# Dense products in unsplit single precision instead of three reduced-precision products

## The reference

```python
def swiglu(h, w_gate, w_up, w_down):          # 1024 x 2816, 1024 x 2816, 2816 x 1024
    return (jax.nn.silu(h @ w_gate) * (h @ w_up)) @ w_down

for i in range(DEPTH):                        # DEPTH = 2
    x = x + 0.5 * swiglu(rmsnorm(x, ffn1_norm[i]), ...)
    x = x + mixer(rmsnorm(x, mix_norm[i]))    # gla: h @ w_in (1024 x 3088), attention, o @ w_out; sb: 1024 x 3072
    x = x + 0.5 * swiglu(rmsnorm(x, ffn2_norm[i]), ...)
# second block: h @ w_in (1024 x 3072), convolution and attention, @ w_out, then
for g in range(G):                            # 4 groups of 8 experts, 1024 x 512 each
    act = jax.nn.silu(hg) * hu * comb[:, g, :, None]
    y = y + jnp.einsum('tef,efd->td', act, w_down[g])
```

## Time and profile before

| | us |
|---|---|
| median of 3 runs | 1604.49 (1604.26 to 1605.66) |
| profiled execution | 1602.25 |
| its span, first to last instruction | 1600.5 |
| TensorE matmuls, busy | 1436.0 (90%) |
| VectorE busy | 885.6 (55%) |
| ScalarE busy | 625.0 (39%) |

### The profile page before, as it was taken

How to read it: one execution, slowest core, us unless ns; L and a number is a source line. 1 busy time by engine, 2 the same in 40 slices (tenths; PEclk the granted TensorE clock), 3 DMA queues, 4 the chain that set the end, 5 groups by cost and what they waited for, 6 DMA issues and landing times.

```text
span 1600.5 us, 23763 instructions
## 1 busy us (share of the span) xinstructions
PE 1436.0 (90%) x9182; PEld 1123.0 (70%) x9182; DVE 885.6 (55%) x1194; ACT 625.0 (39%) x832; POOL 31.0 (2%) x69
## 2 busy tenths in 40 slices
PE   7999999999999999999999999998786767767676
PEld 5888888888888888877788888777643433433433
DVE  4777678577776777665457776786521121121121
ACT  5443465564446434466554434664111011011010
POOL 4000000000000000000010000010000000000000
PEclk9999999999999999999999999999799898888978
DMA  7655543456564655653366554565999999999997
GB/s 220 210 187 197 190 161 132 133 182 211 175 202 148 207 200 171 209 171 119 109 186 210 195 198 158 168 201 224 372 399 416 419 417 417 419 418 417 419 417 309
DMA packets 170770, 396.63 MB, mean 248 GB/s; under 512 B 9508, under 2 KB 107892, under 8 KB 154337
## 3 DMA queue, kind: packets, MB, share of 16 engines
q1 hardware_dynamic: 169152, 392.20, 66.7%
q0 software_dynamic: 1440, 3.72, 1.0%
q10 hardware_dynamic: 128, 0.03, 0.0%
HBM read 393.83 MB, written 1.05 MB: 247 GB/s over the span
## 4 chain that ended last, share of the span: by engine, by line
PE 73%; DMA 11%; SPq 9%; DVE 3%; ACT 2%; issue 1%; DVEq 0%; ACTq 0%
PE psum L518 17%; PE psum L257 12%; PE psum L259 12%; PE psum L258 12%; DMA pair_ring<-in_w_exp_up 9%; PE psum L524 9%; SPq L2210 8%; PE psum L2262 4%; PE psum L2287 2%; PE psum L2306 1%; DMA pair_ring<-in_w_exp_down 1%; PE psum L985 1%; DVE low L252 1%; DVE hT L422 1%; PE psum L1396 1%
## 5 line engine op out<-in xcount | busy, mean ns | idle before, releaser
L252 DVE TENSOR_TENSOR low<-raw,high 128x2048 fp32r<-128x2048 f32 x179 | 409.6, 2291 | 194.2 <-ACT high L248 193.7
L248 ACT ACTIVATE high<-raw 128x2048 fp32r<-128x2048 f32 x179 | 341.3, 1910 | 125.7 <-PE psum L524 89.8
L518 PE MATMUL psum<-hT,high 128*128 128x512 f32 x1152 | 288.0, 392 | 2.0 <-DVE low L252 2.0
L518 PEld LDWEIGHTS psum<-hT,high 128*128 128x128 f32 x1152 | 209.2, 189 | 41.2 <-DVE low L252 2.2
L257 PE MATMUL psum<-high,hT 128*128 128x512 f32 x496 | 201.4, 406 | 8.6 <-DVE low L2546 5.0
L259 PE MATMUL psum<-high,hT 128*128 128x512 f32 x496 | 195.9, 395 | 0.0
L258 PE MATMUL psum<-low,hT 128*128 128x512 f32 x496 | 195.4, 394 | 0.0
L2287 PE MATMUL psum<-pair_ring,scratch 128*32 128x256 f32 x1984 | 139.4, 432 | 55.5 <-DMA pair_ring<-in_w_exp_up 55.4
L524 PEld LDWEIGHTS psum<-hT,low 128*128 128x128 f32 x1152 | 157.1, 190 | 11.3
L524 PE MATMUL psum<-hT,low 128*128 128x256 f32 x1152 | 160.6, 282 | 0.0
L2287 PEld LDWEIGHTS psum<-pair_ring,scratch 128*32 128x32 f32 x1984 | 66.9, 121 | 123.8 <-DMA pair_ring<-in_w_exp_up 68.7
(11 more groups left out here) (336 smaller groups left out, 1482.1 us busy)
## 6 DMA issues: line engine op xcount, KB each, us to landing
pair_ring<-in_w_exp_down SPq DMA_DIRECT2D x64, 1024.0 KB, 22.4
pair_ring<-in_w_exp_gate SPq DMA_DIRECT2D x62, 1024.0 KB, 22.1
pair_ring<-in_w_exp_up SPq DMA_DIRECT2D x62, 1024.0 KB, 22.8
raw<-in_ffn_w_gate SPq DMA_DIRECT2D x88, 512.0 KB, 4.0
raw<-in_ffn_w_up SPq DMA_DIRECT2D x88, 512.0 KB, 5.0
raw<-in_ffn_w_down SPq DMA_DIRECT2D x88, 512.0 KB, 4.3
raw<-in_gla_w_in SPq DMA_DIRECT2D x24, 512.0 KB, 4.5
raw<-in_sb_w_in SPq DMA_DIRECT2D x24, 512.0 KB, 4.7
```

What stands on the lines that cost most here:

```text
L248: act.activation(high[:, p % RING, :], raw_of(p), ACT.Copy).then_inc(rounded, 1)
L252: dve.tensor_tensor(low[:, p % RING, :], raw_of(p), high[:, p % RING, :].bitcast(F32), ALU.subtract).then_inc(split, 1)
L518: pe.matmul(to.rearrange("p (o n) -> p o n", o=2), w_high, both_parts, start=kk == 0, stop=False, skip_group_check=True)
```

## The change

- The type `fp32r`, the buffers `low` and `high`, the second halves of `hT` and `aT` and the split copies of the small weights are gone; two unused buffers keep the addresses behind them. `product` is one matmul in single precision that reads the landed piece.
- `raw` has six slots instead of three. Its loads wait on `used`, the end of the product six pieces before; TensorE waits for the landing of a piece itself. Loops over chunks take two chunks per pass, since six pieces make a round of the ring.
- Turning x: ScalarE writes the first four of eight columns, VectorE the other four, both from PSUM, instead of one after the other.
- The turned gate and up products write 256 columns and `block_norm` reads them from PSUM; copy and add are gone, and `block_gate` writes `aT` directly after waiting for the down products before.
- Experts: slots 0 to 2 lie in space that is free early, the other three wait for pieces 176, 178 and 180; a wait for a pair is one for each of its two DMAs; result adds and stores are made in halves of 512 columns.

```diff
-RING = 3
+RING = 6
+UNROLL = RING // 3
-        low = sb("low", [P, RING, SLOT], F32R)
-        high = sb("high", [P, RING, SLOT], F32R)
         raw = sb("raw", [P, RING, SLOT])
+        spare = sb("spare", [P, SPARE, SLOT])
...
         def piece_loads(sp, p, r, parts):
             if p >= RING or not isinstance(r, int):
-                sp.wait_ge(split, p - RING + 1 + scales_with(r, 3))
+                sp.wait_ge(used, p - RING + 1 + scales_with(r, RING))
...
-        def round_piece(act, p, r=0):
...
-        def split_piece(dve, p, r=0):
...
-        def product(pe, psum_out, lhs_high, lhs_low, rhs_high, rhs_low, start, stop=False):
-
-            pe.matmul(psum_out, lhs_high, rhs_high, start=start, stop=False, skip_group_check=True)
-            pe.matmul(psum_out, lhs_high, rhs_low, start=False, stop=False, skip_group_check=True)
-            return pe.matmul(psum_out, lhs_low, rhs_high, start=False, stop=stop, skip_group_check=True)
-
+        def piece_there(pe, p, r=0):
+            pe.wait_ge(*landed_of(p, r))
+
+        def product(pe, psum_out, lhs, rhs, start, stop=False):
+            return pe.matmul(psum_out, lhs, rhs, start=start, stop=stop, skip_group_check=True)
...
         def x_turn_act(act, k, tt):
...
+            x_turned(act, k, tt, 0)
+            for kk in range(4):
...
         def x_turn_dve(dve, k, tt):
...
+            x_turned(dve, k, tt, 1)
+            for i in range(4):
...
         def gate_up_turned_pe(pe, q, half, c):
...
-                both_parts = hT[:, :, kk * TOKENS:(kk + 1) * TOKENS]
...
             for k in range(4):
                 kk = 4 * half + k
                 for i in range(2):
-                    _, w_low, to = block(k, i)
-                    ins = pe.matmul(to[:, 0:TOKENS], w_low, hT_high[:, kk, :], start=False, stop=kk == KD - 1,
-                                    skip_group_check=True)
+                    cols = slice(i * CHUNK + c * P, i * CHUNK + (c + 1) * P)
+                    ins = product(pe, BLOCK[c][:, i * BANK:i * BANK + TOKENS], four_k(q)[:, k, cols], hT[:, kk, :],
+                                  start=kk == 0, stop=kk == KD - 1)
...
-            def block_sum(n, counter, value, lows):
+            def block_norm(n, counter, value, inner_free):
                 dve.wait_ge(counter, value)
                 if n == 0:
-                    dve.wait_ge(a_low, lows)
+                    dve.wait_ge(a_ready, inner_free)
                 parts = BLOCK[n].rearrange("p (w i n) -> p w i n", w=2, i=2)
...
+            def block_gate(n, number, down_done):
                 dve.wait_ge(block_silu, number + n)
...
+                if n == 0:
+                    dve.wait_ge(used, down_done)
+                ins = dve.tensor_tensor(aT[:, n, :], inner_sb[:, n, 0:TOKENS], inner_sb[:, n, TOKENS:2 * TOKENS], ALU.mult)
...
             for i in range(PAIRS):
-                if i == 1:
-                    sp.wait_ge(split, MOE)
-                elif i == 3:
-                    sp.wait_ge(used, MOE)
+                if i >= 3:
+                    sp.wait_ge(used, MOE - 10 + 2 * i)
                 pair_load(sp, i, 0, i // 3)
...
                 for tt in range(TT):
-                    dve.wait_ge(e["scattered"], b * TT + (tt + 1))
-                    dve.tensor_tensor(x[:, tt, :], SPREAD_Y[tt], x[:, tt, :], ALU.add).then_inc(e["added"], 1)
+                    for j in range(2):
+                        c = slice(j * BANK, (j + 1) * BANK)
+                        dve.wait_ge(e["scattered"], b * 2 * TT + (2 * tt + j + 1))
+                        dve.tensor_tensor(x[:, tt, c], SPREAD_Y[tt][:, c], x[:, tt, c], ALU.add).then_inc(e["added"], 1)
```

More of the change, by code:

```diff
@@ L440, in first_products, with tail_act @@
                 products(j, 1)
-        def tail_act(act, k, first, second, between):
-            round_piece(act, first)
+        def tail_act(act, k, between):
             if k == 7:
@@ L496, in gate_up_pe @@
             for k in range(4):
-                if isinstance(q, int) and q == 0 and tt == 0 and k == 2:
-                    pe.wait_ge(split, 1)
                 kk, tok = 4 * half + k, slice(tt * P, (tt + 1) * P)
-                ins = product(pe, GU[tt], hT_high[:, kk, tok], hT_low[:, kk, tok], four_k(high, q)[:, k, :],
-                              four_k(low, q)[:, k, :], start=kk == 0, stop=kk == KD - 1)
+                ins = product(pe, GU[tt], hT[:, kk, tok], four_k(q)[:, k, :], start=kk == 0, stop=kk == KD - 1)
             if tt == 1:
@@ L592, in first @@
             def first(half, tt):
-                if b + half == 0 and tt == 0:
-                    pe.wait_ge(first_split, 1)
-                else:
-                    pe.wait_ge(split, b + half + 1)
+                piece_there(pe, b + half)
                 gate_up_pe(pe, b + half, half, tt)
@@ L1268, in gla_dve @@
             diff(2)
-            piece(6)
             keep(0)
@@ L1281, in gla_dve @@
             diff(6)
-            piece(8)
             keep(4)
@@ L1321, in gla_dve @@
                 dve.tensor_tensor(v, v, proj[:, tt, 2560:3072], ALU.mult).then_inc(h_ready, 1)
-            piece(14)
-            for tt in range(TT):
-                low_half(tt, 1)
+            turned_tile(1, 1)
             out_dve(dve, "gla_out", 2)
@@ L1770, in mix_act @@
                                bias=eps[:, :]).then_inc(m["root"], 1)
-            piece(14)
-            for tt in range(TT):
-                high_half(tt, 1, tt + 3)
+            turned_tile(1)
             out_act(act, "mix_out", 8)
@@ L1902, in mix_dve @@
             dve.wait_ge(used, b + IN_PIECES)
-            for tt in range(TT):
-                low_half(tt, 0, tt + 1)
-            piece(13)
+            turned_tile(0)
             for tt in range(TT):
@@ L1918, in mix_dve @@
                 ins.then_inc(h_ready, 1)
-            piece(14)
-            for tt in range(TT):
-                low_half(tt, 1, tt + 3)
+            turned_tile(1)
             out_dve(dve, "mix_out", 8)
@@ L2149, in products @@
                 for k in range(4 * half, 4 * half + 4):
-                    tok = slice(tt * P, (tt + 1) * P)
-                    pe.matmul(ROUTE[:, tt * 2 * n:(tt + 1) * 2 * n], hT_high[:, k, tok],
-                              router_parts[:, k, :, :].rearrange("p i n -> p (i n)"), start=tt == 0 and k == 0, stop=False,
-                              skip_group_check=True)
-                    ins = pe.matmul(ROUTE[:, tt * 2 * n:tt * 2 * n + n], hT_low[:, k, tok], router_high[:, k, :],
-                                    start=False, stop=False, skip_group_check=True)
+                    ins = product(pe, ROUTE[:, tt * n:(tt + 1) * n], hT[:, k, tt * P:(tt + 1) * P], router[:, k, :],
+                                  start=tt == 0 and k == 0, stop=k == KD - 1)
                 if half == 1 and tt == 1:
@@ L2280, in gate_up @@
                         pe.wait_ge(e["x_sb"], at(b, 2, half + 1))
-                    pair_there(pe, i, b)
+                    for part in range(2):
+                        half_there(pe, i, b, part)
                     w = pair(i, b).rearrange("p (w k n) -> p w k n", w=2, k=4)
```

520 lines of the change are left out of this document (164 added, 356 removed).

## The result

The changed kernel takes 1830.05 us (median; 1828.99 to 1833.01) against 1604.61 for the kernel before, a ratio of 1.1407 (95% interval 1.1387 to 1.1426): 14% slower. The forecast was 1833, in a range of 1816 to 1862. The profiled span is 1828.4 us; the prediction's sum gave 1828.7. That nearness is partly luck: two of its terms were wrong, in opposite directions. (The other 3 us of the forecast are the step from span to median: the profiled execution had been 2.2 us under the median before, and is level with it now.)

What follows compares the result with a forecast made beforehand. TensorE was taken to bound the dense part, weight loads the experts' part. Span 1600.5 + 244.3 (products) - 13.1 (waits) - 3 (experts and end) = 1828.7 us, so a median of 1833, range 1816 to 1862.

Steps and rivals of the forecast that it cites:

- The price of a product: On TensorE, one single-precision product costs 0.856 us (512 columns) or 0.431 (256), against 0.684 and 0.348: together +244.3 us.
- What the waits gave back: TensorE's waits at the start, for split pieces, at the seventh norm and at the convolution's end shrink: together -13.1 us.
- The start: First product needs four scaled copies and a landed piece, no split; it starts between 8.2 and 9.2 us: -3.1.
- The waits for split pieces: TensorE's waits of 2.0 and 2.4 us for split pieces in dense products go: -4.4 us.
- The norm of index 7: Wait for normalised x (3.5 us in two): next products cover 0.7 more of each, -1.1 (bounds 0 and -3.5).
- The end of the convolution's part: TensorE's waits of 2.06 and 1.11 us and slow matmuls shrink as VectorE loses splits: -4.5 (bounds 0 and -4.5).
- The ring and the new waits: Slots refill five pieces ahead, covering a 4.0 us landing; the gated product's new write is covered too: no new wait.
- Experts and end: Waiting for halves, halved result adds and stores, and fewer routing steps: -3 us (bounds -1 and -5).
- (a): Rival: surplus of about 0.014 us per record comes from the dense loop, not the format: +56, 1889 us; chance 0.07.
- (b): Rival: a single-precision record streams once, so a product of 512 columns costs 0.456 us: 1266 us; chance 0.03.
- (c): Rival: the clock in the dense part ends at 0.86 instead of 1.00, 219 us more: 2052 us; chance 0.03.
- (d): Rival: nothing moves; something else than TensorE sets the dense pace or products compile to the same work: 1604; chance 0.01.

Runs made afterwards that it cites:

- the kernel of streams: A separate kernel computing nothing of the reference, seven streams of 96 matmuls on TensorE; 512 columns took 0.858 us in single precision, 0.229 in reduced.

## Why the prediction was right, and where it wasn't

**The bound: right.** It was read from PE busy 100.00 of 100 beside DVE 71. The run with both products exchanged but the splitting kept (+240 us) and the one with side work added (+0.7 in the medians) show it from both sides.

**The price of a product: right to 3 us.** Forecast 0.856 and 0.431, measured in the loop 0.859 and 0.4316, and the same distances inside the streams. By the loop's numbers and 2.8 for the 40 small products the term is 848 x 0.175 + 1152 x 0.0836 + 2.8 = 247.5 instead of 244.3. The counts by halves show it also apart: +96.8 and +143.2. Rows of a far place, with two operands of the same shape, were good prices.

**What the waits gave back: too low.** Up to the gather the forecast was 13.1; the trace has 247.5 - 226.7 = 20.8. Of it, 12.4 is idle time that went (the table above). The other 8.4 is that PE busy grew less than the price says. Of that, 1.4 is the six cold matmuls of the earlier trace rows, now at full clock, and 1.3 lies at the start of the kernel, which the prediction didn't look at. The timelines of TensorE there, before and after:

```profile
12.35 0.63 PE L258 MATMUL psum<-low,hT 128*128 128x512 f32 x1
...
17.04 1.43 PE L402 MATMUL psum<-ident,x 128*128 128x128 f32 x8
```

```profile
13.10 1.04 PE L391 MATMUL psum<-ident,x 128*128 128x128 f32 x8
```

Before, the first twelve matmuls take 17.04 - 11.78 = 5.26 us instead of the later 2.73; after, the first four products take 13.10 - 8.10 = 5.00 instead of 3.43, and the turning of x behind them is 0.3 us shorter. How long this slow entry lasts differs between profiles (6.55 us for the same four products in the run with three slots). Of the other 5.8 us, 1.2 is spread over the four feed-forward blocks. The rest stands where dense products alternate with other matmuls: 2.0 more in the second block's mixer (busy +19.0, price +22.4), 1.2 in the stick-breaking stage (+21.2, price +22.4), 1.3 around the router and 0.1 in linear attention. In the stick-breaking stage most of it is the switches. In 21 places a dense product stands right behind another kind of matmul; there the first of three matmuls takes 0.32 us instead of 0.23 and the last before such a place 0.26, so a switch cost the old form 0.13 us and costs the new one 0.08. The mixer and the router weren't taken apart. By parts:

- The start: -3.7 measured, -3.1 forecast. The first product starts at 8.10 us, just below the forecast's lower bound of 8.2. The timelines of ScalarE and TensorE show that it waits for the landing of the first piece, not for ScalarE's four copies, which end at 7.83:

```profile
6.69 1.14 ACT L406 ACTIVATE hT<-psum,gainT 128x128 f32<-128x128 f32 x4
```

```profile
8.10 5.16 PE L240 MATMUL psum<-raw,hT 128*128 128x512 f32 x8 [1.72 <-DMA raw<-in_ffn_w_up]
```

- The waits for split pieces, 4.4: gone, nothing in their place. (With both products single and the splitting kept, 1.2 of it was left: longer products alone cover the rest.)
- The norm of index 7: 3.5 to 0.7 us, so -2.8 where the forecast was -1.1. The step allowed only for cover by longer products of 0.7 us each (which is 1.4 for two, not 1.1). The runs with the 848 products in single precision both show 1.5 us, so longer products cover 2.0 and the rest of the change 0.8. The value lies inside its bound.
- The end of the convolution's part: forecast -4.5 with the wait of 2.06 gone; measured about -2.2: the second wait fell from 1.11 to 0.31 and the cold 1.4 went, but the wait of 2.06 is there unchanged, and this step's reason was wrong. (The second wait was for VectorE's low half of the turned h, made behind ScalarE's high half; now each engine copies one tile straight from PSUM. With the low half kept and the products single, it was 1.1 us as before.) It said that VectorE was late because of splits. The timelines of ScalarE, VectorE and TensorE after the change:

```profile
1308.12 0.69 ACT L1529 ACTIVATE proj<-psum,rstd 128x512 f32<-128x512 f32 x1 [2.75 <-PE psum L240]
1308.71 1.05 ACT L1568 ACTIVATE proj<-proj 128x1024 f32<-128x1024 f32 x1
1309.78 1.28 ACT L1570 ACT_TABLE_LOAD   x1
```

```profile
1309.79 1.22 DVE L1690 TENSOR_REDUCE levels<-proj 128x16 f32<-128x1024 f32 x1 [12.53 <-ACT proj L1568]
...
1311.70 1.22 DVE L1696 TENSOR_TENSOR h<-h,levels 128x1024 f32<-128x1024 f32 x1
```

```profile
1312.98 1.09 PE L1483 MATMUL psum<-ident,h 128*128 128x128 f32 x8 [2.06 <-DVE h L1696]
1314.38 5.85 PE L240 MATMUL psum<-raw,hT 128*128 128x512 f32 x13 [0.31 <-ACT hT L1574]
```

VectorE had been idle for 12.53 us, and the wait is as long as before, where it was idle for 1.31. It waits for ScalarE's squares (L1568), ScalarE stands behind its copy of the last input product (L1529), and that waits for TensorE. The chain hangs on TensorE's own last product, so it moves with TensorE, whatever VectorE does. That it is this order is shown by the run with the root ahead of the copies, where the wait is gone. In the kernel with both products single and the splitting kept, the wait was 2.1 too: the splits had no part in it.

**The ring and the new waits: right.** One wait of TensorE for a piece (1.7 us, the first), none for the gated product's new wait. The cover was larger than the argument needed: three slots do as well.

**Experts and end: sized wrong.** Forecast -3, measured +1.2. The tail itself did what was said: from the first matmul of the last scatter to the end it was 1600.5 - 1592.28 = 8.22 us before and 1828.4 - 1821.57 = 6.83 after, -1.4, and the same edits on the kernel before gave 2.2 us. But the rest of this part is paced by weight loads, and its length varies: over the six kernels with the old tail it was 468.4 to 470.3 us (mean 469.7), over the five with the new one 466.9 to 469.6 (mean 468.5), the shortest with the edits on the kernel before. The kernel before was the shortest of its six and the changed kernel the longest of its five, so the +1.2 is no finding of its own: the means differ by -1.2, and a term of -3 taken from one profile is of the size of the spread. Why VectorE's and TensorE's steps there, which hardly changed, don't make the loads run closer wasn't tried.

**The rivals.** (a), a surplus in the dense loop: 0.859 in the loop, 0.858 alone; refuted. (b), a record that streams once: refuted by 0.858. The Trainium skill, Perfetto Trace Analysis, Engine Utilization, halves the output rate for this format, as the prediction named it; read for a whole product, this trace doesn't agree: a product leaves two records of 0.429 us each, so its rate is about a quarter of the reduced matmul's. (c): the clock of the dense windows is 1.00. (d): the difference is 14%. The price is the format's.

The two errors that count, 7.7 us too little for idle and small savings and 4.2 too much for the experts and the end, with 3.2 for the price between them, cancel to 0.3 in the span (3.2 - 7.7 + 4.2). The range would have held the time without that. (Its two ends are not the sums of the bounds named for them, which give 1820 and 1870; the time lies inside those too.)

## What to carry to other kernels

Take the cost of a format from the start-to-start distance of the records in a full stream, not from the count of instructions or of multiplications: three reduced-precision matmuls (0.684 us for 512 columns) beat one in single precision (0.858), and the rounding and splitting they need is free as long as TensorE covers it. Before pricing a wait at zero, follow its releaser back to the start: a chain that hangs on the waiting engine's own last result moves with it, and emptying the engine in the middle gives nothing. And where loads set the pace of a stage, an edit worth 3 us there is hard to see in one profile.

## What the runs showed of the hardware

- Single precision on TensorE leaves two records of weight load and matmul for each product, and costs 0.858, 0.430 and 0.222 us for 512, 256 and 128 columns: in proportion to the columns, with about 4% on top at 128.
- A reduced-precision matmul over 512 columns takes 0.229 us, not half of a single-precision record's 0.429 (0.214), and it does so with the same weights, too. Inside a stream it is 0.2267 against 0.2146, with new weights or the same, with copies beside it or without: the 0.012 us are neither new weights nor this traffic on SBUF.
- Copies of ScalarE and VectorE beside a full stream cost TensorE nothing measurable, with VectorE at 44% and ScalarE at 33% busy (0.859 us a product), with VectorE at 62% (230.40 us a feed-forward block with and without), and in the reduced stream (0.2267 us beside the copies and after them).
- The first matmuls after idle stood 0.43 us apart for 512 columns instead of 0.23, eleven of them in the kernel of streams and twelve at the start of the kernel before, while the view of windows gives the clock there as 1.00.
